# The order of the query tiles in the second attention: 3, 2, 1, 0 against 3, 0, 2, 1

## The reference, cut to what matters

```
ss = einsum('bgrqd,bgqnkd->bgrqnk', qb, k_sel) - slopes * d_s        # selected
sw = einsum('bgrqd,bgkd->bgrqk', qb, kwb) - slopes * d_w             # windowed
o_s, o_w = softmax(ss) @ v_sel, softmax(sw) @ vwb                    # causal
return gb[0] * o_c + gb[1] * o_s + gb[2] * o_w
```

## Time and profile before

| What | us |
|---|---|
| Median of 3 runs (3127.45 to 3128.27) | 3127.89 |
| Profiled execution | 3130.95 |
| Its span | 3129.1 |
| PE busy, of the span | 3052.0 |
| DVE busy | 1723.4 |
| ACT busy | 1060.0 |
| POOL busy | 291.5 |
| Second attention, from the first scores to the last values | 2612 to 2704.5 |

### The profile page before, as it was taken

How to read it: one execution, slowest core, us unless ns; L and a number is a source line. 1 busy time by engine, 2 the same in 40 slices (tenths; PEclk the granted TensorE clock), 3 DMA queues, 4 the chain that set the end, 5 groups by cost and what they waited for, 6 DMA issues and landing times. The chain is left out here.

```text
span 3129.1 us, 39351 instructions
## 1 busy us (share of the span) xinstructions
PE 3052.0 (98%) x13548; PEld 2449.2 (78%) x13548; DVE 1723.4 (55%) x2469; ACT 1060.0 (34%) x1630; POOL 291.5 (9%) x236
## 2 busy tenths in 40 slices
PE   8999999999999999999999999999999799989999
PEld 6888888778888887888878877888888575668887
DVE  6555564565654556555456365555546767453334
ACT  4222323342332235322232333232224545542223
POOL 1000200000200023000020000200003215500000
PEclk9999999999999999999999999999999898999999
DMA  4232222113323222432232212333222320012222
GB/s 185 96 136 98 88 100 90 42 53 111 141 94 141 96 84 86 152 134 101 86 103 94 69 42 74 111 141 138 98 94 81 148 72 21 34 68 95 100 94 80
DMA packets 87961, 303.13 MB, mean 97 GB/s; under 512 B 10400, under 2 KB 20768, under 8 KB 86688
## 3 DMA queue, kind: packets, MB, share of 16 engines
q1 hardware_dynamic: 87840, 301.59, 27.4%
HBM read 299.45 MB, written 2.10 MB: 96 GB/s over the span
## 5 line engine op out<-in xcount | busy, mean ns | idle before, releaser
L1026 PE MATMUL proj<-u_hi,w_hi 128*128 128x512 f32 x2616 | 1029.4, 394 | 27.7 <-DVE u_lo L1435 21.1
L1028 PE MATMUL proj<-u_hi,w_lo 128*128 128x512 f32 x2616 | 1020.7, 390 | 0.0
L1027 PE MATMUL proj<-u_lo,w_hi 128*128 128x512 f32 x2616 | 1020.6, 390 | 0.0
L1430 DVE TENSOR_TENSOR w_lo<-raw,w_hi 128x1024 fp32r<-128x1024 f32 (+4 forms) x575 | 657.8, 1147 | 499.6 <-ACT w_hi L610 492.3
L610 ACT ACTIVATE w_hi<-raw 128x1024 fp32r<-128x1024 f32 (+4 forms) x575 | 538.0, 948 | 356.9 <-PE proj L1028 232.2
L1026 PEld LDWEIGHTS proj<-u_hi,w_hi 128*128 128x128 f32 x2616 | 492.5, 188 | 143.0 <-DVE u_lo L1435 27.3
L1027 PEld LDWEIGHTS proj<-u_lo,w_hi 128*128 128x128 f32 x2616 | 492.9, 188 | 104.1 <-issue 3.4
L1028 PEld LDWEIGHTS proj<-u_hi,w_lo 128*128 128x128 f32 x2616 | 492.6, 188 | 103.4
L1026 PE MATMUL proj<-a_hi,w_hi 128*128 128x512 f32 x960 | 379.9, 396 | 1.6 <-DVE a_lo L1727 0.9
L1028 PE MATMUL proj<-a_hi,w_lo 128*128 128x512 f32 x960 | 374.1, 390 | 0.0
L1027 PE MATMUL proj<-a_lo,w_hi 128*128 128x512 f32 x960 | 373.8, 389 | 0.0
(11 more groups left out here) (399 smaller groups left out, 2835.3 us busy)
## 6 DMA issues: line engine op xcount, KB each, us to landing
raw<-in_ffn_gu SPq DMA_DIRECT2D x174, 512.0 KB, 3.5
raw<-in_in_w SPq DMA_DIRECT2D x68, 512.0 KB, 3.4
raw<-in_ffn_dn SPq DMA_DIRECT2D x64, 512.0 KB, 3.4
raw<-in_ff SPq DMA_DIRECT2D x64, 512.0 KB, 3.5
gate<-in_ada SPq DMA_DIRECT2D x8, 3072.0 KB, 11.5
raw<-in_ffn_dn SPq DMA_DIRECT2D x32, 384.0 KB, 3.0
raw<-in_in SPq DMA_DIRECT2D x18, 512.0 KB, 3.5
raw<-in_mla_out SPq DMA_DIRECT2D x16, 512.0 KB, 3.4
```

The lines of the kernel that those rows point to most:

```text
L1026: pe.matmul(out, w_h, x_h, start=first, stop=False)
L1027: pe.matmul(out, w_h, x_l, start=False, stop=False)
L1028: return pe.matmul(out, w_l, x_h, start=False, stop=last)
L1430: dve.tensor_tensor(wt(w_lo, slot, slot.tiles), wt(raw, slot, slot.tiles), wt(w_hi, slot, slot.tiles).bitcast(F32), ALU.subtract).then_inc ...
```

## The change

The tiles of a head pair are taken in the order qt = 3, 0, 2, 1, so that the widths are 512, 128, 384, 256. The width of `prob` (L329), which was written out for the falling order, now comes from `step`. Nothing else differs: the same instructions on the same engines, with other sizes at each place in the list, and all the waits count as before.

```diff
         def step(g):
 
-            j, qt = g // QT, QT - 1 - g % QT
+            j, qt = g // QT, (3, 0, 2, 1)[g % QT]
             return j, qt, (qt + 1) * P
 
-        prob = lambda g, i: p_buf[4 * (g % 3) + i][:, 0:(QT - g % QT) * P]
+        prob = lambda g, i: p_buf[4 * (g % 3) + i][:, 0:step(g)[2]]
```

## The result

| | before | after |
|---|---|---|
| Median of 5 runs, us | 3128.27 (3127.45 to 3129.69) | 3139.40 (3134.44 to 3144.58) |
| Ratio to before, 95% interval | | 1.0032 (1.0022 to 1.0043) |
| Profiled execution, us | 3130.95 | 3135.94 |
| First scores to last values in it, us | 2612.1 to 2703.6 | 2612.1 to 2709.3 |

The change costs 0.32%, 11.1 us by the medians. Forecast were 7.1 us and 3135.0; the median is 4.4 us above that and inside the range of 3131 to 3142. One thing stands out before any trace is opened: the five times of before lie within 2.2 us, those of after within 10.1. It is compared with before first, and the scatter later.

A forecast was written before the change was run, and what follows sets the result against it. PE and POOL, both nearly full in the second attention, set the pace through a ring. POOL's gaps go from 3.10 to 10.1 us, 7.0 more, 7.1 with the end; on 3127.89 that gives 3135.0 us, range 3131 to 3142.

The forecast's parts named there:

- The ring: Second attention: POOL finishes step g-3, PE transposes it and scores g, DVE and ACT make g's factors, POOL begins g.
- the third step of a pair: Step with `values` in front, 384 wide after the change: POOL idle 3.26 us in steps 6, 10 and 14.
- the two steps of cover: POOL's work on the two steps before the third: 8.48 us after the change, against 11.74 needed.
- the first pair's: POOL's gap at the third step of the first pair, without `values` in front: 0.3 us, bounds 0 to 1.09.
- the 0.61, 1.09 and 0.79: POOL's old gaps, 0.61 twice ahead of 512 wide steps, 1.09 and 0.79 early on: claimed to go, 3.10 us together.
- my own case: POOL's gaps lengthen the second attention, PE's clock holding in the middle pairs: 3132.5 to 3138 us, chance 0.62.
- rival 1: PE's clock falls ahead of `values` in one to three pairs, 3.7 us each: 3138 to 3146 us, chance 0.25.
- a stretch 72% busy: PE's sparse transposes and narrow scores ahead of `values`, worked out about 72% busy; whether the clock falls there left open.
- The price of a fall: Both branches of `values` at the low clock, 9.3 us in place of 5.6: 3.7 us in the ring each time.
- The end: POOL's last step 256 wide in place of 128 adds 0.15 us; last pair's `values` at the low clock as before.
- The rule on transposes: Form of rival 1: transposes not counting as activity, clock falls in all three pairs, 3146.1 us; 0.05 of rival 1's chance.
- Rival 2: POOL's two steps cover the third, so it runs without a gap and old gaps are saved: 3124.9 us, chance 0.10.

The follow-up runs named there:

- third order: Query tiles in the order 2, 0, 3, 1 (widths 384, 128, 512, 256), against the changed kernel's 3, 0, 2, 1; 3142.7 us, 1.0045 of before.
- the unaltered change: The changed kernel (order 3, 0, 2, 1) run once more with nothing altered; 3141.7 us, 1.0042 of before.
- the last two: Two more single executions of the changed kernel, nothing altered, each profiled; 3139.9 and 3134.3 us.
- the fill: Changed kernel with score matmuls of the 512 wide step (branch 0) and 128 wide step (both branches) issued twice; 3136.5 us, 1.0021 of before.

## Why the prediction was right, point by point

*Where the time goes: right.* The ring, the third step of a pair, the two steps of cover were named; the gap came to 3.24 (3.26 forecast), the first pair's to 0.21 (0.3), the period to 20.26 (20.3), the 0.61, 1.09 and 0.79 went, and the last values began 7.26 us later (7.1). Leaving out values showed the ring one to one, and a third order gave 4.75 for 4.8. Each term of the working was a start-to-start time of a dense stretch, not a busy time.

*The size of the median: short by 4 us.* The term that was off is of PE's clock: the sum put falls in the three middle pairs at nothing. The median of 3139.4 lies outside the interval of my own case (3132.5 to 3138) and in that of rival 1 (3138 to 3146); the range of 3131 to 3142 held because it also took in executions with one fall, and there was luck in it. The sum was for an execution without falls; of the twelve times of the unaltered change, four are at 3134.3 to 3135.9, as it says, and eight at 3139.4 to 3145.1. The mean granted clocks on record fit: 0.988 or 0.989 in the four, 0.986 to 0.988 in the eight, the lowest in the longest. Rival 1 was thus not the exception with 0.25 but the commoner case. I weighed it by a stretch 72% busy between 88% that held and 55% that fell, and took "above any with which it fell" for an argument. Stretches of the same list fell in one execution and held in another (the last two, for example), which a single trace of before could not show. The price of a fall came out near, 3.3 us in the ring for 3.7 forecast, but of other parts: forecast were both branches of values at the low clock, measured were the scores of step 6 (1.47 us in place of 0.85) and branch 0 alone (5.97 in place of 3.31), while branch 1 was back at the full clock. That a fall goes with such an excess of POOL's gap is shown in one execution of this kernel and one of the third order (4.3 us there); that falls explain all eight is inferred, from the fill, which took 5.2 us off the median and halved the scatter, and from the clocks.

*The end: a small error the other way.* I took the last values to be at the low clock throughout, 9.3 us. They nearly were in the execution with the fall (9.2 us); in the profile after and in the other single execution they took 7.7. So at full clock in the pairs the stage lost 5.8 us and not 7.1.

*The rule on transposes.* By the Trainium skill ("TensorE: Matmul & The Clock Gate", Part 4: PE-mode transpose) transposes do not count as activity as other matmuls do, and I worked out three falls in each execution from it. The profile after has none, nor have two others of this kernel: PEclk is 1.00 in 2660.80 to 2681.10, with 40 transposes among waits for POOL. For these fp32 transposes the measurement decides against three certain falls; whether a transpose counts for less than another matmul it cannot tell.

*Rival 2* (the bridge holds) had its deciding point at 8.48 us of cover and less than 0.9 of gap; 3.24 was measured. What I had not seen: the cover has a second customer. The next step's `biased` on DVE stands ahead of the factors, and with a wide next step the gap moves to the first step of the pair, 0.96 in the order 2, 3, 1, 0.

## What to carry to other kernels

Where two engines are both nearly full and hand work around a ring, alternating wide and narrow pieces is not what balances them: ask what work the waiting engine has in its queue when a lump (here the values) passes through the other, and put the widest pieces just ahead of the lump. A reordering that adds no instruction can still open small waits on PE, and here these were paid twice, once as waits and, in some executions, once as a falling clock. That shows as scatter between executions and not in one profile: compare the mean granted clocks of a kernel's executions. Relief of the second full engine gained more than any order (5.9 us for a quarter of POOL's tiles moved), but half of its tiles was too many for the engine that took them.

## What the runs showed of the hardware

DVE and POOL slowed each other when both scaled tiles in SBUF. From the kernel with two tiles on DVE, in step 8 (start, length):

```profile
2659.92 0.49 DVE L1971 TENSOR_SCALAR work<-work,row_stats 128x512 f32<-128x512 f32 x1
2659.98 1.86 POOL L590 TENSOR_SCALAR work<-work,row_stats 128x512 f32<-128x512 f32 x1 [2.48 <-DVE row_stats L1968]
2660.32 0.92 DVE L1971 TENSOR_SCALAR ux<-ux,row_stats 128x512 f32<-128x512 f32 x1
2661.81 1.56 POOL L590 TENSOR_SCALAR ux<-ux,row_stats 128x512 f32<-128x512 f32 x1
```

The same instruction takes 0.49 and then 0.92 us on DVE, and POOL's takes 1.86 beside it and 1.56 after. The Trainium skill ("GPSIMD Engine Reference", 8. Key points) says that GpSimd shares its SBUF interfaces with VectorE and that some kinds of DVE instruction contend with it; the rows agree with that, but which kind it is was not tried. With the kernels as they were, DVE's `biased` and copies ran beside POOL all the time, and its 512 wide tile stayed at 1.56.
